# SSD sums of squares: sixteen short products on TensorE, or adds on GpSimd and one product at the end

## What is computed

```python
    y = (y_fwd + y_bwd + d_skip[:, None] * xs).reshape(b, t, BRANCH_WIDTH)
    y = rmsnorm(y * jax.nn.silu(z[..., :BRANCH_WIDTH]), norm_g)
```

## Time and profile before

| | us |
|---|---|
| median of 3 runs | 2143.9 |
| lowest, highest | 2143.15, 2144.04 |
| span of the profiled execution | 2143.2 |
| PE busy | 2099.4 (98%) |
| DVE busy | 1089.1 (51%) |
| POOL busy | 924.6 (43%) |
| ACT busy | 800.1 (37%) |

### The profile page before, as it was taken

One profiled execution on the slowest core, in us unless ns is written; L12 is line 12 of the kernel. 1 busy time (PEld: TensorE's weight loads), 2 busy tenths in 40 slices (PEclk: granted clock), 3 DMA queues, 4 the chain that ended last, 5 costly groups with the idle time before them and its releaser, 6 DMA issues.

```text
span 2143.2 us, 31195 instructions
## 1 busy us (share of the span) xinstructions
PE 2099.4 (98%) x12580; PEld 1789.7 (84%) x12580; DVE 1089.1 (51%) x1866; ACT 800.1 (37%) x1943; POOL 924.6 (43%) x623
## 2 busy tenths in 40 slices
PE   8999999999999999999999999999999999999997
PEld 7888887788898888787788887888888888888885
DVE  4104332598898898897712233144333423541447
ACT  4123122465464555473322111143424323432343
POOL 5533332333343343325742332654454445544544
PEclk9999999999999999999999999999999999999999
DMA  5221112335232233235331111322131223123213
GB/s 189 90 68 53 51 50 74 137 98 143 80 109 80 70 118 100 78 119 173 125 125 50 50 50 50 96 87 68 59 88 59 68 59 96 40 68 86 69 50 118
DMA packets 206685, 184.19 MB, mean 86 GB/s; under 512 B 23916, under 2 KB 172684, under 8 KB 206541
## 3 DMA queue, kind: packets, MB, share of 16 engines
q1 hardware_dynamic: 206541, 182.20, 27.7%
HBM read 168.19 MB, written 12.21 MB: 84 GB/s over the span
## 4 chain that ended last, share of the span: by engine, by line
PE 50%; DVE 4%; issue 1%; ACT 0%; DMA 0%; POOL 0%; DVEq 0%; POOLq 0%; ACTq 0%
PE bank L214 25%; PE bank L264 9%; PE bank L574 6%; PE bank L2411 2%; PE bank L2439 2%; PE bank L1067 2%; PE bank L2422 2%; PE bank L1093 1%; DVE acc L944 1%; PE bank L1131 1%; DVE acc L940 1%; DMA R<-macc_dram 0%; PE bank L447 0%; DVE R L422 0%; PE bank L2483 0%
## 5 line engine op out<-in xcount | busy, mean ns | idle before, releaser
L188 POOL TENSOR_SCALAR Wh<-Wraw 128x1024 fp32r<-128x1024 f32 x217 | 245.9, 1133 | 1100.2 <-issue 755.2
L214 PE MATMUL bank<-Hh,Wh 128*128 128x512 f32 (+1 forms) x1936 | 664.6, 343 | 3.2 <-ACT R L817 1.4
L214 PE MATMUL bank<-Hl,Wh 128*128 128x512 f32 (+1 forms) x1936 | 652.0, 337 | 0.0
L214 PE MATMUL bank<-Hh,Wl 128*128 128x512 f32 (+1 forms) x1936 | 651.0, 336 | 0.0
L191 POOL TENSOR_TENSOR Wl<-Wraw,Wh 128x1024 fp32r<-128x1024 f32 x217 | 550.6, 2537 | 18.1
L214 PEld LDWEIGHTS bank<-Hh,Wh 128*128 128x128 f32 x1936 | 367.7, 190 | 51.0 <-issue 10.8
L214 PEld LDWEIGHTS bank<-Hh,Wl 128*128 128x128 f32 x1936 | 367.3, 190 | 39.0
L214 PEld LDWEIGHTS bank<-Hl,Wh 128*128 128x128 f32 x1936 | 367.9, 190 | 36.6 <-issue 1.7
L298 DVE TENSOR_TENSOR acc<-bank,acc 128x512 f32<-128x512 f32 x240 | 165.0, 690 | 166.3 <-PE bank L264 165.5
L264 PE MATMUL bank<-Wh,Mh 128*128 128x512 f32 x528 | 208.7, 395 | 8.7 <-DVE acc L298 7.6
L264 PE MATMUL bank<-Wh,Ml 128*128 128x512 f32 x528 | 205.7, 390 | 0.0
(11 more groups left out here) (259 smaller groups left out, 3124.0 us busy)
## 6 DMA issues: line engine op xcount, KB each, us to landing
Wraw<-in_na_w_in_dram SPq DMA_DIRECT2D x80, 512.0 KB, 3.8
Wraw<-in_ssd_w_in_dram SPq DMA_DIRECT2D x57, 512.0 KB, 4.2
Wraw<-in_w_out_dram SPq DMA_DIRECT2D x48, 512.0 KB, 3.3
R<-acs_dram SPq DMA_DIRECT2D x16, 1536.0 KB, 6.8
Wraw<-in_w_mem_kv_dram SPq DMA_DIRECT2D x32, 512.0 KB, 3.9
R<-gs_dram SPq DMA_DIRECT2D x32, 128.0 KB, 3.5
R<-R SPq DMA_DIRECT2D x32, 128.0 KB, 3.6
macc_dram<-acc SPq DMA_DIRECT2D x1, 3072.0 KB, 11.5
```

Source lines behind the costliest of these rows:

```text
L188: pool.tensor_scalar(Wh[:, s, :], Wraw[:, s, :], 1.0, 1.0, ALU.mult, ALU.mult).then_inc(pool_c, 1)
L214: mm = pe.matmul(DB[h.k % 2][:, 0:t1 - t0], w[:, k, :], x[:, k, t0:t1], start=(k == 0 and i == 0), stop=(k == KC - 1 and i == 2))
```

## The change

ACT writes the squares of pair 0 into a new buffer `pre.sq` of 768 columns. For pairs 1 to 14 it writes them into z as before, and POOL adds z to `pre.sq` in place (`add_squares`). POOL does the add of pair n after the split of the second unit of pair n + 1; it waits there for the squares and for its own add before. PE has no squares within the loop any more. After the first two tiles of the last output units it multiplies both `pre.sq` and z (which holds pair 15's squares) by ones, accumulating in 6 columns: 12 products. DVE copies 6 columns where it added up 96. ACT's wait before it overwrites z is now for POOL's add of the pair before.

```diff
--- before.py
+++ after.py
@@ -1174,7 +1174,8 @@
             def window(self, r):
 
                 at, r.at = r.at, 0
-                self.ab, self.cs, self.xx, self.spare = r(2, 2, T), r(2, 2, 4, P), r(3, NT, P), r(2 * PAIRS)
+                self.ab, self.cs, self.xx, self.sq, self.spare = r(2, 2, T), r(2, 2, 4, P), r(3, NT, P), r(T), r(2 * PAIRS)
+                assert r.at <= at
                 r.at = at
                 mark = r.at
                 self.raw, self.conv = r(2, T + 6), r(2, T + 2)
@@ -1576,8 +1577,19 @@
 
             def gpsimd(pool):
                 chain(pool, "pool")
-                for _ in range(unit_index(PAIRS) - 4 + 2):
+
+                def add_squares(n):
+
+                    pool.wait_ge(sq_done, n + 1)
+                    if n > 1:
+                        pool.wait_ge(sq_summed, n - 1)
+                    pool.tensor_tensor(pre.sq, pre.sq, z, ALU.add).then_inc(sq_summed, 1)
+
+                behind = {unit_index(n + 1) + 1: n for n in range(1, LAST)}
+                for u in range(4, unit_index(PAIRS) + 2):
                     split_unit(pool)
+                    if u in behind:
+                        add_squares(behind[u])
 
             def scalar(act):
                 take_raw, silu = pre.takes(act)
@@ -1654,7 +1666,7 @@
                     decay()
                     begin_table(ACT.Silu)
                     if n == LAST:
-                        act.wait_ge(sq_summed, n)
+                        act.wait_ge(sq_summed, n - 1)
                         take_spans(act, z, ACT.Silu)
                         U["act"].next()
 
@@ -1670,8 +1682,8 @@
                         take_raw(j + 1, conv_row(*extra[0]))
                         silu(j, n + 1, xs[1 - a])
                     if n < LAST:
-                        if n:
-                            act.wait_ge(sq_summed, n)
+                        if n > 1:
+                            act.wait_ge(sq_summed, n - 1)
                         take_spans(act, z, ACT.Silu)
                     if out_in(n):
                         forward(n + 1)
@@ -1688,7 +1700,7 @@
                         silu(j + 1, conv_row(kind, group), bT if kind == "b" else cT[group % 2])
 
                     def square():
-                        act.activation(z, y, ACT.Square).then_inc(sq_done, 1)
+                        act.activation(z if n else pre.sq, y, ACT.Square).then_inc(sq_done, 1)
 
                     if n == LAST:
                         act.wait_ge(ab_exp, PAIRS)
@@ -1884,8 +1896,7 @@
                             nxt.mem_norm.dve_normed(dve, 2 + k)
                     dve_out_tiles(dve, half, (4, 5))
                     if half == 0:
-                        dve.tensor_reduce(ssum, A[0][:, 256:256 + PAIRS * NT].rearrange("p (n i) -> p i n", i=NT), AXX,
-                                          ALU.add).then_inc(reduced, 1)
+                        dve.tensor_copy(ssum, A[0][:, 256:256 + NT]).then_inc(reduced, 1)
                 HF["dve"].k = half0 + 2 * dense_index(PAIRS)
                 dve.wait_ge(rooted, 1)
                 c.link(dve.reciprocal(rssd[:, :], sd))
@@ -1921,27 +1932,21 @@
                         mm = pe.transpose(chunk(A[2:4], ch), xs[n % 2][:, ch * P:(ch + 1) * P], ident[:, :])
                     mm.then_inc(x_turned, 1)
 
-                def squares(n, signal=sq_summed):
-                    pe.wait_ge(sq_done, n + 1)
+                def squares():
+                    pe.wait_ge(sq_done, PAIRS)
+                    pe.wait_ge(sq_summed, LAST - 1)
                     for i in range(NT):
-                        mm = pe.matmul(A[0][:, 256 + n * NT + i:257 + n * NT + i], z[:, i * P:(i + 1) * P],
-                                       ones[:, 0:1], start=True, stop=True)
-                    mm.then_inc(signal, 1)
+                        for k, sq in enumerate((pre.sq, z)):
+                            mm = pe.matmul(A[0][:, 256 + i:257 + i], sq[:, i * P:(i + 1) * P], ones[:, 0:1],
+                                           start=(k == 0), stop=(k == 1))
+                    mm.then_inc(summed, 1)
 
                 turn_b(0)
                 group_bc(0)
                 for n in range(PAIRS):
                     g, a = n // 4, n % 2
 
-                    if n < LAST:
-                        pe_dense(pe, between=lambda: turn_x(n))
-                    else:
-
-                        def between():
-                            turn_x(n)
-                            squares(n - 1)
-
-                        pe_dense(pe, between=between)
+                    pe_dense(pe, between=lambda: turn_x(n))
 
                     pe.wait_ge(x_scaled, n + 1)
                     pe.wait_ge(x_copied, n + 1)
@@ -1952,8 +1957,6 @@
                                            xw[:, d, src[s], :], start=True, stop=True)
                     mm.then_inc(states_done, 1)
                     pe.wait_ge(cb_taken, g + 1)
-                    if 0 < n < LAST:
-                        squares(n - 1)
                     if next_group(n):
                         turn_b(g + 1)
                     if n < LAST:
@@ -1992,7 +1995,7 @@
                     for k in range(2):
                         pe_out_tiles(pe, (2 * k, 2 * k + 1), last_mix)
                         if half == k == 0:
-                            squares(LAST, summed)
+                            squares()
                         nxt.mem_norm.pe(pe, 2 * half + k)
                     pe_out_tiles(pe, (4, 5), last_mix)
 
```

## The result

The changed kernel takes 2185.1 us, the median of 5 runs (2184.1 to 2187.8), against 2143.9 us for the kernel before (now 5 runs, 2143.2 to 2147.5): a ratio of 1.0191, 95% interval 1.0178 to 1.0203. It is slower by 41.2 us; 10.5 had been forecast, and the range ended at 2161.

The account below looks back on a forecast made before the run. DVE was taken to bound the phase from 440 to 990 us; collisions and moved splits, summed by stretch, gave +10.5 us on the median of 2143.9: 2154.4 us, slower at 0.63, with an 8-in-10 range of 2139 to 2161.

Parts of the forecast that it names:

- What bounds the kernel: From 440 to 990 us DVE, not PE with its 98% busy, is the tighter engine; PE could gain 0.2 us in pairs 5 and 6.
- rivals 1 to 3: PE bounds (2126 us, 0.05), part of the gain comes through (2138 to 2141, 0.12), or a wash (2143 to 2148, 0.2).
- rival 2: Part of the gain comes through in pairs 3, 4, 7 and 8, where DVE waits for PE: 2138 to 2141 us; chance 0.12.
- What the change takes from PE: Fourteen calls of squares at 1.26 us leave PE, 17.6 us less work; ACT's wait before z is overwritten costs nothing.
- Rival 4: POOL's add, delayed by waits, makes the split behind it late for PE in pairs 12 and 14: 4 us more; chance 0.04.
- What an add does to DVE: POOL's add collides with DVE's two-SBUF-input instructions, 1.6 to 2.0 us each; six adds in even pairs up to 12 are free.
- What an earlier PE does to the splits: POOL's splits follow PE forward onto other DVE instructions: 0.65 us on L1814, 2.7 us on pair 3's convolution, 1.6 of it hidden.
- The end: The doubled closing products come where PE waits 1.01 us for DVE anyway: +0.2 us.
- the signs that had been listed: PE busy about 17 us lower, squares' passes 192 to 24, waits for DVE some 34 us, L1785 and L1788 1.5 to 2 longer.

Follow-up runs that it names:

- experiment 2: Changed kernel with the last add a split earlier and PE's squares put back: 2160.7 us; changed kernel with neither adds nor squares: 2156.4 us.
- experiment 5: Changed kernel with POOL adding only the squares of even pairs 2 to 12, PE keeping the other squares: 2152.7 us.
- experiment 6: Splits reading one operand, in the kernel before: 2126.0 us; without adds and squares: 2114.1; in the changed kernel with pair 14's add a split earlier: 2119.4.
- experiment 1: Changed kernel with POOL's add of pair 14 behind the split of pair 15's first unit instead of its second: 2176.7 us.
- experiment 7: Closing products in two blocks of 12, in the changed kernel with pair 14's add earlier: 2174.2 us; with products in PE's waits too: 2162.3 us.
- experiment 4: 12 unused products in PE's even-pair waits, added to the changed kernel with pair 14's add earlier: 2164.3 us; to that without adds and squares: 2157.9 us.

## Why the forecast was right in its sign and wrong in its size

**What bounds the kernel**: right. DVE is the tighter engine of the phase. With 17.6 us less work for PE alone pairs 1 to 14 take 8.3 us longer and the kernel 11.8 us (experiment 2), so rivals 1 to 3 fall, and with them the reading of the page by the highest occupancy. Part of rival 2's reason was sound: the adds of the even pairs are free (experiment 5).

**What the change takes from PE**: the work was right, 17.9 us where the clock is undisturbed (experiment 6). The sentence that ACT's wait costs nothing because POOL has long added by then is the first step that failed. It had asked whether the add's input is ready and POOL has time, not what stands ahead of the add in POOL's queue. In pair 15 that is a split whose weights land at 989.41, and it cost 13.0 us, 2.3 of them by the clock behind the long wait (y's products take 5.6 us instead of 3.3). Rival 4 named POOL's queue, but in the other direction, an add that holds a split up, and priced it at 4 us. POOL's idle 299 us, given as evidence against it, was no evidence: in the 19.21 us ahead of that split POOL was idle and blocked.

**What an add does to DVE**: right. 1.85 us for 768 columns (1.8 forecast), +1.4 on the first segment sum in pair 6 (1.5), +1.5 in pair 15 with the add in time (2.0). The Trainium skill, SBUF — State Buffer, section Who interferes with whom, adds that the order of issue decides who blocks. The trace of experiment 1 agrees: the add that starts at 974.02 inside L1797 ends at 976.45, L1797 keeps its 1.75, and L1800 behind it pays with 3.30.

**What an earlier PE does to the splits**: right in kind, mis-sized; this is the second step that failed. For pair 3 the convolution was to grow to 4.17 + 2.7 = 6.87, and took 6.84. But in pair 5 the moved split was booked as cheaper by 0.45; it lies beside the decay products and costs 3.03, less 0.66 on L1814 and 0.68 on the convolution, so +1.7. Through pairs 1 to 14 the loss with PE kept busy, adds and moved splits together, is 15.7 us (table) where 8.3 had been summed.

**TensorE's clock**: no term at all, and no reason given for leaving it out; by its price this is the largest step that failed. The forecast expected PE's waits to grow to some 34 us and took them as the whole price of waiting. Its table by stretch had the granted clock in it, at 1.00 in both stretches of the phase, but no row of before had so many waits. Waiting costs twice when it brings the clock down: 14.1 us in pairs 1 to 14.

**The end**: +0.2 forecast, +1.4 measured. The doubled products bring 1.3 us, of which the wait of 1.01 us hides most, as was said: where the clock stays up behind them the end, up to the late wait, loses 0.1 and 0.3 us in two kernels (experiment 7), though 1.1 in a third, that of experiment 4 with the halving. The clock behind the block of 24 brings the rest.

Together, from the traces: queue 13.0, clock in the pairs 14.1, the rest in the pairs 15.7, pair 15 without the queue 1.5, end 1.4, less 2.6 ahead of pair 0: 43.1, against a difference of the spans of 42.9 us. The sum is put together from the stretches of three profiles, so its closeness is no proof of the single terms.

Of the signs that had been listed, PE's busy time did not fall (clock), the squares' passes went to 24 at the end, the waits for DVE grew to 29.0 us and the long one, L1785 and L1788 grew by 1.0 and 0.0 in pair 2, 1.4 and 0.7 in pairs 6 and 10, and the third tile of pair 6 came at 656.27 instead of 647.95. In pair 14 they did not grow: the add, at 939.36, is itself drawn out to 3.11 us, and L1747 behind it pays 0.8. Pairs 4, 8 and 12, which the list did not name, grew by 1.0 on L1785. In pair 15 the add came 20 us too late to meet them.

What stays open: what, beside the length of a wait, decides that the clock falls behind it, since 3.25 us left it up and 2.44 took it down in one kernel, and since it can fall or stay in the same code. The 1.7 us that the kernel with PE kept busy loses in pair 15 against its partner (3.2 and 1.5) are a case of this: behind waits of 3.39 and 3.42 us ahead of y the clock fell in the first and stayed in the second, and y's products take 4.9 us and 3.3.

## What to carry to other kernels

Where two engines are both near full, take work from the one that the other waits for; work taken from its partner moves the partner's followers, here GpSimd's splits, onto other instructions, and that can cost more than it gave. Before an operation is put into a queue, look at what each instruction ahead of it waits for in every iteration, the last one above all: an idle engine may be a blocked one. And count a new wait of TensorE together with the clock behind it, as a cost that comes in some executions and not in others.

## What the runs showed of the hardware that was not expected

- TensorE fell to its lower level behind its waits of 2.8 to 3.8 us at the third tile in all seven even pairs of the changed kernel, and 12 useless products in such waits made the kernel 12.4 us faster.
- The clock fell in one execution and not in another of the same code: behind a wait of 1.9 us near the end (0.58 in experiment 1, 1.00 in the changed kernel), and at 268 to 272 us with PE busy throughout (0.50 in the kernel before, 1.00 in the changed one).
- 24 one-column passes in 2.73 us, without any wait, left the clock at 0.57 to 0.68 in nine of ten profiles; two blocks of 12 left it at 1.00 in both profiles that have them.
- A GpSimd copy with one operand left the DVE instruction of two that had begun before it at 1.76 us, and was itself held up, 2.22 instead of 0.84 us. Adds made such DVE instructions 2.7 to 3.3 us long.
- A split (both its halves, 3.5 us) beside twelve short DVE instructions of two SBUF operands cost them 3.03 us together; beside one long instruction, L1735, a split had cost up to 2.1.
